# First products between the first modulation blocks, and the delta output projection begun with its ready inputs

## The chip, the cores and the metric

The kernel runs on one core of a Trainium2 chip. The time is device microseconds of one execution; the number that counts is the median of several. Times inside an execution are microseconds from the first instruction of the profiled one.

Engines: PE (TensorE, matrix products), ACT (ScalarE), DVE (VectorE), POOL (GpSimd), SP (SyncE, which here only issues DMA). Each runs its own instructions in order and waits for semaphores that the others raise.

## The reference

Two transformer blocks over 512 latent tokens of width 1024 (the first block also carries 256 context tokens, 768 columns in all), everything in float32. Only two places matter here. The start of the first block, layer 0 of 2:

```python
shift, scale, gate = jnp.split((c_act @ w_mod + b_mod)[:, None, :], 3, axis=-1)
lat = split_cols((rms_norm(h, norm_g) * (1.0 + scale) + shift) @ w_in)
```

(the same for the context with its own vector), and, in the second block, the end of the gated delta branch and the output projection of its mixing stage:

```python
o = o * lax.rsqrt(jnp.mean(o * o, axis=-1, keepdims=True) + EPS) * g_out
o = o * jax.nn.silu(gate)
mix = jnp.concatenate([attn_o, dn_o], axis=-1) @ w_out[l]
```

Half of the input of that last product, `attn_o`, is the window attention's output and has been finished long before the delta recurrence ends.

## The kernel before, in words

**Layout.** The stream is held with the 1024 features on 8 tiles of 128 partitions and the tokens in the free dimension. A weight chunk is 128 x 1024 float32 (512 KB): the eight 128 x 128 blocks that make one output tile. SP streams all chunks through `ring`, five places, in a fixed order; chunk c goes out only when chunk c - 5 is used (`chunk_used`). The order at the start is: parameters, chunk 0, all constants (1089 KB), then chunks 1 to 4 alternating with the four quarters of the tokens (768 KB each), then chunks as places come free.

**Split products.** A product is made exact enough by three passes: weights and inputs are split in a rounded "lead" and a rest, and PE adds lead x lead, lead x rest and rest x lead. The weight's lead is an ACT copy (`weight_leads`, L736) into one of two places of `scratch` or, for a few chunks in `LEAD_SPOTS`, a place of its own; its rest is a POOL subtraction in place (L564). A lead in `scratch` must wait until the chunk that used the place before is done. The input's split is a DVE cast (L1247) and subtraction (L1249), or an ACT copy (L761) and a DVE subtraction (L1474).

**The start.** Sixteen chunks hold the shift and scale columns of `w_mod`. A block b is two chunks. For each, PE makes two `modulation_part`s (L1995, a row of 256 sums), ACT copies the row out (`modulation_row`, L718), and PE turns it into columns (`modulation_turn`, L2005, which needs the constants). Beside them goes the first norm: ACT squares a token tile (L695), PE sums it over partitions (`norm_step`, L2012). The loop over b has one norm step per block from b = 2 on. After the last, ACT makes the root (L686, L687), and DVE makes the shifts and scales of all tiles at once (`modulation`, L1228 and L1232). Then, for each of the 8 tiles k, DVE multiplies by the root (L1467), ACT applies shift and scale (`modulate`, L757), and the result is split. `project_two` (L1957) makes the first two output tiles of the input projection together, tile k by tile k as the splits arrive, 12 matmuls for each k. Its weights are chunks 20 and 21 of the ring, behind four chunks of later modulation blocks; two of those blocks, of the 16 left, are made ahead of `project_two`.

**The end of the delta branch.** The recurrence has four steps s. After it, ACT squares each of the four heads (L1143), PE sums (L2584, into `pair_ps`), ACT makes the root (L686, L687), and DVE multiplies by root, gain and gate (L1770, L1771) and splits (L1247, L1249). Between the roots ACT makes the leads of the first two output chunks (L736) and POOL their rests. Then comes the output projection "out_2": eight output tiles, each 24 matmuls over eight input tiles (L1900, `project_split`). Input tiles 0 to 3 are the window attention's, 4 to 7 the delta heads. The order of all work is the order in which the code issues it; there is no scheduler.

## Time and profile before

| | us |
|---|---|
| median of 3 runs | 1842.37 |
| lowest, highest | 1839.61, 1842.48 |
| the profiled execution | 1841.66 |
| span of its instructions | 1839.8 |
| mean granted TensorE clock | 0.979 |

A row of the timeline reads: start, duration, engine, line, operation, tile written <- tiles read, shape, count, and in brackets how long the engine had been idle and who released it. A row of the chain of waits reads: start, duration, what the end of the execution hung on in that stretch. "L1957" is line 1957 of the kernel before.

### The profile page before, as it was taken

What the parts mean: (1) busy time and instruction counts of PE and PEld (TensorE: products, weight loads), DVE (VectorE), ACT (ScalarE), POOL (GpSimd) and SP (SyncE); (2) the same over time, 40 slices, a digit from 0 to 9 for tenths busy, and PEclk for the clock granted to TensorE, in tenths of its full rate; (3) what the DMA queues carried; (4) which work ended last, traced back from release to release, by engine and by line L of the source; (5) the groups of instructions that cost most, each with busy time, mean ns of one, the idle gap of its engine ahead of it and who ended that gap; (6) DMA issues with size and microseconds to landing.
All of it is one profiled execution on the core that took longest, in us unless ns stands there. A gap on an engine that the chain in (4) does not pass through costs nothing.

```text
span 1839.8 us, 32525 instructions
## 1 busy us (share of the span) xinstructions
PE 1701.1 (92%) x13658; PEld 1370.7 (74%) x13658; DVE 839.7 (46%) x1513; ACT 712.4 (39%) x1101; POOL 606.2 (33%) x318
## 2 busy tenths in 40 slices
PE   6899999988989989989999988788899899999997
PEld 3788888866878767768877757686688688888886
DVE  0401265475330356476747567574434444444113
ACT  3525213254353524354634966014423522222222
POOL 0222322193323323453034304113235244444443
PEclk9899999999999999999999989999999999999999
DMA  8344311210122111403522200001121132222232
GB/s 335 127 163 146 115 48 47 106 46 13 64 96 69 58 58 59 138 1 102 178 88 92 80 24 2 4 2 54 58 73 47 51 107 95 92 93 102 94 104 78
DMA packets 43721, 152.20 MB, mean 83 GB/s; under 512 B 4544, under 2 KB 7744, under 8 KB 43328
## 3 DMA queue, kind: packets, MB, share of 16 engines
q1 hardware_dynamic: 40032, 140.73, 22.1%
q10 hardware_dynamic: 3552, 9.47, 1.4%
q8 instruction: 108, 1.77, 0.4%
q14 instruction: 29, 0.24, 0.1%
HBM read 145.98 MB, written 4.19 MB: 82 GB/s over the span
## 4 chain that ended last, share of the span: by engine, by line
PE 78%; DVE 11%; ACT 6%; issue 4%; DMA 1%; SPq 0%; POOL 0%; DVEq 0%; ACTq 0%
PE wide_ps L1900 53%; PE wide_ps L1957 4%; PE pair_ps L2012 2%; PE wide_ps L2192 1%; PE wide_ps L1973 1%; PE wide_ps L2495 1%; DVE xn L1383 1%; DMA ring<-weights 1%; DVE xn L1628 1%; DVE proj L1301 1%; PE duo_ps L1995 1%; PE duo_ps L2622 1%; DVE proj L1297 1%; PE wide_ps L2078 1%; PE wide_ps L2603 1%
## 5 line engine op out<-in xcount | busy, mean ns | idle before, releaser
L564 POOL TENSOR_TENSOR ring_r<-ring,scratch_r 128x1024 fp32r<-128x1024 f32 x176 | 430.9, 2449 | 961.9 <-ACT scratch_r L736 887.5
L1900 PE MATMUL wide_ps<-xn_r,scratch_r 128*128 128x512 f32 x1272 | 470.3, 370 | 0.0
L1900 PE MATMUL wide_ps<-work_r,scratch_r 128*128 128x512 f32 (+1 forms) x1109 | 427.5, 386 | 5.2 <-ACT proj L723 5.2
L1900 PE MATMUL wide_ps<-work_r,ring_r 128*128 128x512 f32 (+1 forms) x1109 | 412.6, 372 | 0.0
L736 ACT ACTIVATE scratch_r<-ring 128x1024 fp32r<-128x1024 f32 x192 | 203.6, 1061 | 529.4 <-PE wide_ps L1900 461.5
L1900 PEld LDWEIGHTS wide_ps<-xn_r,scratch_r 128*128 128x128 f32 x1272 | 240.4, 189 | 47.5 <-issue 5.4
L1900 PEld LDWEIGHTS wide_ps<-work_r,scratch_r 128*128 128x128 f32 x1109 | 209.0, 188 | 53.5 <-ACT proj L723 9.9
L1900 PEld LDWEIGHTS wide_ps<-work_r,ring_r 128*128 128x128 f32 x1109 | 209.1, 189 | 38.6
L1900 PE MATMUL wide_ps<-proj_r,scratch_r 128*128 128x512 f32 (+1 forms) x662 | 225.7, 387 | 2.5 <-DVE proj_r L1249 2.5
L1900 PEld LDWEIGHTS wide_ps<-proj_r,scratch_r 128*128 128x128 f32 x662 | 125.4, 190 | 30.7 <-DVE proj_r L1249 3.3
L723 ACT ACTIVATE proj<-wide_ps 128x512 f32<-128x512 f32 (+2 forms) x86 | 56.7, 659 | 208.1 <-PE wide_ps L1900 198.4
L1420 DVE TENSOR_TENSOR work<-work 128x512 f32<-128x512 f32 (+2 forms) x35 | 36.4, 1039 | 124.3 <-ACT work L695 123.5
L1354 DVE SCALAR_TENSOR_TENSOR proj<-proj,par_sb,qe 128x768 f32<-128x768 f32 (+1 forms) x6 | 5.6, 930 | 184.4 <-ACT qe L687 184.4
L1900 PE MATMUL wide_ps<-proj_r,ring_r 128*128 128x512 f32 x188 | 75.0, 399 | 0.0
L1900 PE MATMUL wide_ps<-conv_tmp_r,ring_r 128*128 128x512 f32 (+1 forms) x179 | 66.4, 371 | 0.0
L1900 PE MATMUL wide_ps<-conv_tmp_r,scratch_r 128*128 128x512 f32 (+1 forms) x179 | 66.4, 371 | 0.0
L1440 DVE TENSOR_TENSOR h<-h,work 128x768 f32<-128x768 f32 (+1 forms) x16 | 29.8, 1863 | 65.2 <-ACT work L925 65.2
L1957 PE MATMUL wide_ps<-work_r,proj_r 128*128 128x512 f32 (+1 forms) x98 | 45.4, 463 | 12.4 <-DVE xn_r L1249 10.7
L1247 DVE CAST proj_r<-proj 128x512 fp32r<-128x512 f32 x24 | 51.8, 2160 | 0.8
L1808 DVE TENSOR_TENSOR proj<-wide_ps,work 128x512 f32<-128x512 f32 x30 | 20.6, 691 | 54.9 <-PE wide_ps L1900 38.5
L890 ACT ACTIVATE work<-pair_ps 128x512 f32<-128x512 f32 x52 | 31.0, 598 | 35.8 <-PE pair_ps L2215 35.8
L2215 PE MATMUL pair_ps<-const_sb,xn 128*128 128x128 f32 x208 | 31.2, 286 | 13.8 <-DVE xn L1383 7.8
(442 smaller groups left out, 2972.6 us busy)
## 6 DMA issues: line engine op xcount, KB each, us to landing
ring<-weights SPq DMA_DIRECT2D x256, 512.0 KB, 3.5
h<-tokens SPq DMA_DIRECT2D x4, 768.0 KB, 11.5
h<-tokens ACTq DMA_DIRECT2D x1, 3072.0 KB, 10.0
out<-h ACTq DMA_DIRECT2D x1, 2048.0 KB, 7.2
h<-out ACTq DMA_DIRECT2D x1, 2048.0 KB, 9.2
out<-h SPq DMA_DIRECT2D x16, 128.0 KB, 1.7
const_sb<-const SPq DMA_DIRECT2D x1, 1089.0 KB, 6.0
h<-mem ACTq DMA_DIRECT2D x1, 1024.0 KB, 12.7
```

The costliest lines, as they stand in the source:

```text
L564: pool.tensor_tensor(as_r(wt), wt, as_r(w_lead(m)).bitcast(F32), ALU.subtract).then_inc(w_split, 1)
L723: act.activation(dst, wide_ps[0:rows, g % 2 if bank is None else bank, 0:w], func).then_inc(evacuated, 1)
L736: act.activation(as_r(w_used(stage, w_lead(m))), w_used(stage, ring[:, c % RING, :]), ACT.Copy).then_inc(w_lead_ready, 1)
L890: act.activation(pair_probs_t(p)[:, 512 * q:512 * q + 512], turn_bank(g), ACT.Copy).then_inc(at_pt, 1)
L1247: dve.tensor_copy(as_r(lead), src).then_inc(x_lead, 1)
L1420: dve.tensor_tensor(total, total, squares(n)[:, k % 2, 0:w], ALU.add).then_inc(sq_used, 2 if k == 1 else 1)
L1440: dve.tensor_tensor(h[:, n, 0:w], h[:, n, 0:w], resid[:, n % 2, 0:w], ALU.add).then_inc(h_ready, 1)
L1808: dve.tensor_tensor(dst, proj_bank(stage, tile), root[:, 0:LAT], ALU.mult).then_inc(evacuated, 1)
L1900: last = pe.matmul(bank[:, a:b], wt[:, cols], as_r(x[:, a:b]), start=n == 0 and p == 0, stop=n == len(k_order) - 1 and p == 2)
L1957: last = pe.matmul(ps[:, a:b], wt[:, cols], as_r(x[:, a:b]), start=k == 0 and p == 0, stop=k == KT - 1 and p == 2)
L2012: last = pe.matmul(pair_ps[:, a:b], cst["ones"], squares(n)[:, k % 2, a:b], start=k == 0, stop=k == KT - 1)
L2215: last = pe.transpose(turn_bank(g)[:, t * P:(t + 1) * P], pair_probs(p - 1)[:, 512 * q + t * P:512 * q + (t + 1) * P], cst["ident"])
```

## The change

**Start, columns.** The modulation columns are laid out on the host by tile, so that block b holds shift and scale of token tile b alone. `first_modulation(b)` on DVE makes that tile's numbers as soon as block b is turned, and `modulate` waits for them tile by tile.

**Start, order of PE.** All eight norm steps go between the first three blocks; blocks 3, 4 and 5 follow; blocks 6 and 7 go inside `project_two`, behind its k = 0 and k = 1, and the first two of the later blocks behind k = 4 and k = 6.

**Start, ACT.** `modulation_row` is called for rows 0 and 1 ahead of the first and the fifth square, for 2 and 3 behind the root and the two weight leads, and for 4 to 9 behind tiles 0, 1, 2, 3, 5 and 7 of `modulate`.

**Start, DMA.** Constants go in two parts: 160 KB with identity, ones and the turning columns behind chunk 0, 960 KB with the tables behind chunk 7. The weights of the first two output tiles leave the ring: each has a place in `proj` and a semaphore of its own and is issued behind chunk 5 and chunk 6.

**out_2.** Its first two leads get places of their own in `xn` (`LEAD_SPOTS`), and ACT makes them behind step s = 1 of the recurrence. PE makes output tile 0 over input tiles 0 to 3 ahead of the first two head sums, output tile 1 over the same ahead of the last two, and input tiles 4 to 7 for both together afterwards (`out_part`).

```diff
-    for name, n in ([("mod0", MOD_FIRST), ("proj0", NPROJ + 2 * MIXED), ("dft0", FOURIER_CHUNKS[0]), ("out0", KT),
+    for name, n in ([("mod0", MOD_FIRST), ("proj0", NPROJ - 2 + 2 * MIXED), ("dft0", FOURIER_CHUNKS[0]), ("out0", KT),
...
+        ROWS_BEHIND = {0: 4, 1: 5, 2: 6, 3: 7, 5: KT, 7: KT + 1}
...
                 if c == 0:
-                    sp.dma_start(const[:, :], const_d).then_inc(const_landed, 16)
+                    sp.dma_start(const[:, 0:CONST_HEAD], const_d[:, 0:CONST_HEAD]).then_inc(const_landed, 16)
+                if c in (5, 6):
+                    sp.dma_start(w_home("proj0", c - 5), weights[where("proj0", c - 5)]).then_inc(first_landed[c - 5], 16)
+                if c == 7:
+                    sp.dma_start(const[:, CONST_HEAD:], const_d[:, CONST_HEAD:]).then_inc(tables_landed, 16)
...
             def modulate(ly):
-                act.wait_ge(mod_ready, (2, 4)[ly])
                 for k in range(KT):
-                    if ly == 0 and k == 1:
-                        modulation_row(KT + 1)
-                        weight_leads("proj0", 1)
+                    act.wait_ge(mod_ready, (2 * (k + 1), 2 * KT + 2)[ly])
...
+                    if ly == 0 and k in ROWS_BEHIND:
+                        modulation_row(ROWS_BEHIND[k])
...
                     for k in range(KT):
-                        modulation_row(k)
+                        if k in (0, 4):
+                            modulation_row(k // 4)
                         act.wait_ge(tokens_landed[k // 2], 16)
                         square(0, k, h[:, k, :], TOK)
                     mean_root(0, TOK)
-                    weight_leads("proj0", 0)
-                    modulation_row(KT)
+                    weight_leads("proj0", 0, 2)
+                    modulation_row(2)
+                    modulation_row(3)
...
+                if s == 1:
+                    weight_leads("out_2", 0, 2)
...
-                if n in (1, 2):
-
-                    weight_leads("out_2", n - 1)
...
+            def first_modulation(b):
+
+                dve.wait_ge(mod_turned, b + 1)
...
+            def first_block(b):
+
+                pe.wait_ge(mod_row, b - 1)
+                if b == 4:
+                    pe.wait_ge(root_ready, 1)
                 modulation_part(0, 2 * b)
+                modulation_turn(b - 1)
+                if b == 2:
+                    norm_step(0, 6, TOK)
+                    norm_step(0, 7, TOK)
                 modulation_part(0, 2 * b + 1)
...
+            def behind_first_products(k):
+
+                if k < 2:
+                    first_block(6 + k)
+                elif k == 2:
+                    modulation_turn(KT - 1)
+                elif k == 4:
+                    late_block(KT)
+                elif k == 6:
+                    modulation_turn(KT)
+                    late_block(KT + 1)
...
+            def out_part(tiles, ks):
...
             for n in range(4):
+                if n % 2 == 0:
+                    out_part([n // 2], range(4))
                 pe.wait_ge(do_sq, n + 1)
...
-            for n in range(KT):
-                project_split("out_2", n, range(KT), mix2_lead, lambda k: tile_2[:, MIX2[k], :], LAT, mix2_ready if n == 0 else None)
+            out_part([0, 1], range(4, KT))
+            for n in range(2, KT):
+                project_split("out_2", n, range(KT), mix2_lead, lambda k: tile_2[:, MIX2[k], :], LAT)
```

On PE, the program's start before (L1995 is a half block, L2005 a turn, L2012 a norm step in two matmuls, of 512 and of 256 columns):

```order
L1995 MATMUL wide_ps<-ring,state 32x256 x12
L2005 MATMUL duo_ps<-const_sb,work 128x2 x2
L1995 MATMUL wide_ps<-ring,state 32x256 x8
L2005 MATMUL duo_ps<-const_sb,work 128x2 x2
L1995 MATMUL wide_ps<-ring,state 32x256 x4
L2012 MATMUL pair_ps<-work,const_sb 128x512
L2012 MATMUL pair_ps<-work,const_sb 128x256
L1995 MATMUL wide_ps<-ring,state 32x256 x4
L2005 MATMUL duo_ps<-const_sb,work 128x2 x2
L1995 MATMUL wide_ps<-ring,state 32x256 x4
```

and now (L2037, L2049 and L2056 are the same three):

```order
L2037 MATMUL wide_ps<-ring,state 32x256 x8
L2056 MATMUL pair_ps<-work,const_sb 128x512
L2056 MATMUL pair_ps<-work,const_sb 128x256
L2056 MATMUL pair_ps<-work,const_sb 128x512
L2056 MATMUL pair_ps<-work,const_sb 128x256
L2037 MATMUL wide_ps<-ring,state 32x256 x4
L2049 MATMUL duo_ps<-const_sb,proj 128x2 x2
L2056 MATMUL pair_ps<-work,const_sb 128x512
L2056 MATMUL pair_ps<-work,const_sb 128x256
L2056 MATMUL pair_ps<-work,const_sb 128x512
L2056 MATMUL pair_ps<-work,const_sb 128x256
L2037 MATMUL wide_ps<-ring,state 32x256 x4
```

The norm steps now stand two at a time ahead of half blocks that they stood behind.

On ACT, from the root of the first norm to the fourth token tile of `modulate`, now (L709 and L710 the root, L765 the weight leads, L741 the copy of a row, L783 the modulation of a tile in two pieces, L787 its lead):

```order
L709 ACTIVATE work<-pair_ps,eps 128x768 [waits sq_used]
L710 ACTIVATE work<-work 128x768 [waits act_chain]
L765 ACTIVATE proj_r<-proj 128x1024 [waits first_landed0]
L765 ACTIVATE proj_r<-proj 128x1024 [waits first_landed1]
L741 ACTIVATE proj<-wide_ps 128x256 [waits mod_turned,chunk_used] x2
L783 ACTIVATE xn<-xn,small 128x512 [waits scaled,mod_ready]
L783 ACTIVATE xn<-xn,small 128x256
L741 ACTIVATE proj<-pair_ps 128x256 [waits mod_turned,chunk_used]
L783 ACTIVATE xn<-xn,small 128x512 [waits scaled,mod_ready]
L783 ACTIVATE xn<-xn,small 128x256
L787 ACTIVATE work_r<-xn 128x768 [waits xn_ready]
L741 ACTIVATE proj<-pair_ps 128x256 [waits mod_turned,chunk_used]
```

Before, rows 0 to 7 were all copied ahead of L709; now six of them stand behind it.

On PE, the end of the recurrence before (L2577 its last products, L2584 the head sums, L1900 the projection):

```order
L2577 MATMUL duo_ps<-work,xn 128x128 x8
L2584 MATMUL pair_ps<-work,const_sb 128x512 x4
L1900 MATMUL wide_ps<-proj_r,scratch_r 128x512 x2
L1900 MATMUL wide_ps<-proj_r,ring_r 128x512
L1900 MATMUL wide_ps<-proj_r,scratch_r 128x512 x2
```

and now (L2654, L2679 and L2668 the same; the rows from the third are output tile 0 over input tiles 0 to 3):

```order
L2654 MATMUL duo_ps<-work,xn 128x128 x8
L2668 MATMUL wide_ps<-proj_r,xn_r 128x512 x2
L2668 MATMUL wide_ps<-proj_r,ring_r 128x512
L2668 MATMUL wide_ps<-proj_r,xn_r 128x512 x2
L2668 MATMUL wide_ps<-proj_r,ring_r 128x512
L2668 MATMUL wide_ps<-state_r,xn_r 128x512
L2668 MATMUL wide_ps<-proj_r,xn_r 128x512
L2668 MATMUL wide_ps<-state_r,ring_r 128x512
L2668 MATMUL wide_ps<-qe_r,xn_r 128x512
L2668 MATMUL wide_ps<-proj_r,xn_r 128x512
L2668 MATMUL wide_ps<-qe_r,ring_r 128x512
L2679 MATMUL pair_ps<-work,const_sb 128x512 x2
```

Twelve products of output tile 0 stand ahead of the first head sum, twelve of tile 1 ahead of the third.

## Rows read from the trace of the kernel before

**Rows 1.** The page: busy time of the engines, share of the span, instructions.

```profile
PE 1701.1 (92%) x13658; PEld 1370.7 (74%) x13658; DVE 839.7 (46%) x1513; ACT 712.4 (39%) x1101; POOL 606.2 (33%) x318
```

**Rows 2.** Chain of waits, 0 to 75 us: start, duration, what (x counts trace records).

```profile
6.46 15.37 DMA ring<-weights
...
21.88 1.08 PE wide_ps L1995 x8
22.96 2.58 PE pair_ps L2012 x4
25.53 0.57 PE wide_ps L1995 x8
26.10 0.54 PE duo_ps L2005 x4
...
27.21 1.49 PE pair_ps L2012 x4
...
44.41 0.91 ACT work L686
...
53.85 19.45 PE wide_ps L1957 x96
```

**Rows 3.** Timeline of PE, its last two waits before the first products.

```profile
47.46 0.61 PE L2005 MATMUL duo_ps<-const_sb,proj 128*128 128x2 f32 x4 [2.08 <-ACT proj L718]
...
53.85 0.77 PE L1957 MATMUL wide_ps<-work_r,proj_r 128*128 128x512 f32 x1 [4.79 <-DVE xn_r L1249]
```

**Rows 4.** Timeline of ACT, 45 to 53 us.

```profile
45.34 0.84 ACT L687 ACTIVATE work<-work 128x768 f32<-128x768 f32 x1
46.09 1.04 ACT L736 ACTIVATE proj_r<-ring 128x1024 fp32r<-128x1024 f32 x1
47.04 0.36 ACT L718 ACTIVATE proj<-duo_ps 128x256 f32<-128x256 f32 x1
47.30 1.30 ACT L757 ACTIVATE xn<-xn,small 128x512 f32<-128x512 f32 x2
...
51.69 0.85 ACT L761 ACTIVATE work_r<-xn 128x768 fp32r<-128x768 f32 x1
```

**Rows 5.** Timeline of DVE, 46 to 58 us.

```profile
46.22 1.83 DVE L1467 TENSOR_TENSOR xn<-h,work 128x768 f32<-128x768 f32 x2 [4.09 <-ACT work L687]
48.64 2.05 DVE L1247 CAST work_r<-xn 128x768 fp32r<-128x768 f32 x1 [0.59 <-ACT xn L757]
50.72 2.99 DVE L1249 TENSOR_TENSOR xn_r<-xn,work_r 128x768 fp32r<-128x768 f32 x1
...
56.23 0.55 DVE L1247 CAST conv_tmp_r<-xn 128x768 fp32r<-128x768 f32 x1
56.82 0.96 DVE L1249 TENSOR_TENSOR xn_r<-xn,conv_tmp_r 128x768 fp32r<-128x768 f32 x1
```

**Rows 6.** Timeline of POOL, its first weight rest.

```profile
47.21 3.05 POOL L564 TENSOR_TENSOR ring_r<-ring,proj_r 128x1024 fp32r<-128x1024 f32 x1 [45.99 <-ACT proj_r L736]
```

**Rows 7.** Windows of PE: stretch, length, PE busy (records), granted clock, DMA share, GB/s.

```profile
53.85:57.83 3.98, 3.98 (x13) 0.50 0.02 4
57.83:61.63 3.80, 3.80 (x20) 0.81 0.00 0
```

**Rows 8.** Chain of waits, 1240 to 1304 us.

```profile
1240.17 1.86 PE duo_ps L2577 x16
...
1243.46 1.14 PE pair_ps L2584 x2
...
1247.52 2.48 DVE proj_r L1247
...
1250.03 2.72 DVE proj_r L1249
...
1260.54 41.45 PE wide_ps L1900 x171
```

**Rows 9.** Line L1808, DVE reading PSUM: count, ns min/median/max, first and last start.

```profile
L1808 DVE TENSOR_TENSOR proj<-wide_ps,work x30: 678/692/692, 1330.5 to 1698.8; 128x512 f32<-128x512 f32 x30
```

157 lines of the change are left out of this document (104 added, 53 removed).

## The prediction, made before the changed kernel had run

> **What bounds the kernel now.** The busy shares come first: PE works 92% of the span, no other engine half of it [rows 1]. So the time is PE's work plus PE's waits, and an edit is worth what it takes out of those waits (or of stretches at the lower clock) and nothing else. The chain of waits then says where they lie. In the first 54 us it leaves PE three times [rows 2]. First for the DMA: chunk 5, issued at 6.46, lands 15.37 us later, behind all constants and tokens. Then for the root at 44.41, after a run of PE work that is continuous from 21.88. Then for the first input tile: the products of `project_two` start at 53.85, after idle times of 2.08 and 4.79 us [rows 3], and run 19.45 us to 73.30. Windows of PE show the price behind the second wait: granted clock 0.50 for the first 3.98 us, which hold the 12 matmuls of k = 0, and 0.81 in the next [rows 7]. At the end of the recurrence PE finishes at 1242.03 and the full stream of the output projection starts at 1260.54 [rows 8]; between them stand squares, sums, roots and a DVE chain, in which a cast takes 2.48 us and a subtraction 2.72.
>
> **Prices, from rows.** Half block 0.57 us at the high clock (1.08 at the low one), turn 0.54, norm step 1.49 (2.58 low) [rows 2]. ACT: root 0.91 + 0.84, weight lead 1.04, row copy 0.36, modulating a tile 1.30, its lead 0.85 [rows 2, 4]. DVE: root product 1.83 / 2 = 0.92, cast 0.55, subtraction 0.96 [rows 5]. One k of `project_two`: 3.98 at the low clock [rows 7]; at the high one (73.30 - 61.63) / 5.5 = 2.12, since 61.63 lies half way through k = 2 [rows 2, 7].
>
> **Start, until the root.** The first constants shrink from 1089 to 160 KB. Up to chunk 5 the queue moved about 7.5 MB by 21.83, or 0.37 MB per us [rows 2]; 0.95 MB less puts the last tokens and chunk 5 about 2.6 us earlier, near 18 and 19. The two first weight chunks follow at about 20.6 and 23.4. PE can sum tiles 0 and 1 from about 10 us on, at the low clock (to 15), then half block 2, norm steps 2 and 3, half block 3 (to 20.1). ACT holds row 1 until that half block is done, so square 4 ends at 21.5; steps 4 and 5 end at 24.5, half block 4 and turn 1 at 25.6, steps 6 and 7 at 28.6, half block 5 at 29.2. Root: 28.6 + 0.91 + 0.84 = **30.4**, against 46.2 before. Fifteen us earlier, but not fifteen us won, since blocks 3 to 7 are still to come.
>
> **From the root to the first products.** ACT queues two weight leads ahead of row 2: it is out at 30.4 + 2.1 + 0.4 = 32.8. PE has finished half block 6 at 29.8 and waits 3.0 us for it: a wait that the change adds, with all blocks queued behind it. Then turn 2, half blocks 7 and 8, turn 3 (35.1), half blocks 9 and 10 (36.2), turn 4 (behind row 4, which stands behind `modulate` of tile 0, out at 36.2), half block 11 at 37.3. For the input: DVE multiplies tile 0 to 31.4, then waits for turn 2 to make tile 2's scales, then turn 3 for tile 3's; ACT has tile 0 at 35.8. POOL meanwhile makes the two weight rests. Before, DVE's cast took 2.05 instead of 0.55 and its subtraction 2.99 instead of 0.96 exactly while POOL ran [rows 5, 6]: the two stop each other. Here POOL runs from 31.5 to about 37.3, so the cast of tile 0 starts then, and its split is ready at **39.0**. PE waits 1.7 us. It would be 37.6 without the collision.
>
> **Inside `project_two`.** Eight k at 2.12 are 17.0. Added to it: blocks 6 and 7 (4 x 0.57), turns 5, 6, 7 (3 x 0.54), two later blocks (2 x 1.1) and their turn (0.4), in all 6.5. These are no new work, only moved. Two waits more. Row 8 stands on ACT behind the later block that PE makes after k = 4; tile 6 is modulated only behind it (ACT 54.9 to 56.2), cast and subtracted by 57.8, while PE has finished k = 5 at 56.5: 1.3 us. DVE has eight small instructions more than before in the loop, 0.4 us for each tile, which hold splits back by a few tenths (k = 4) that fit in the same sum: 0.2. End of the products: 39.0 + 17.0 + 6.5 + 1.3 = **63.8** (the turn that follows at 73.30 before follows here too). Before it was 73.30, with the same work done by then. **Gain 9.5 us.** What follows is PE without a break, so the shift lasts. The wait for the tables (landed near 27) costs nothing, nor do the ring's waits: chunk 12 can go out at 34 with half block 7, and is needed at 41.
>
> Bounds of this term: without the POOL collision +1.4, with a little less waiting in the loop 11.2. The clock: after the wait of 2.08 us PE went on at the high level, after 4.79 at the low one [rows 2, 3, 7]; the new one of 3.0 lies between. If the clock falls there and again at 37, half blocks and turns cost 2 us more and k = 0 1.9 us more: 5.6. The rise before took most of 5.4 us of products. I take the high level, as the gap is nearer to 2.08.
> On this, the Trainium skill ("TensorE: Matmul & The Clock Gate", section "What's actually happening") says that throttled is the default and that activity releases it. By that rule alone either level can stand after 3.0 us; it would put the gain between 5.6 and 9.5.
>
> **out_2.** Before, from the end of the recurrence: output of the last step on DVE, square, head sum 1.14, root, then for each head about 2.6 us on DVE, of which head 0 lost (2.48 - 0.44) + (2.72 - 0.69) = 4.1 to POOL's two weight rests [rows 8]. Output tile 0 hung on head 3's split until 1260.54, and then came 171 matmuls in 41.45 us: 0.232 each at the high clock, 39.7, and 1.7 for a start at the low one.
> Now PE puts 12 matmuls (2.8 us) ahead of head sum 0, which then ends at 1245.8 instead of 1244.6: 1.2 lost on DVE's chain, since the square is ready at 1243.4. ACT has no leads between the roots, and POOL is quiet: head 0 is split at 1249.8 (1252.75 before), head 1 at 1252.4. Head sums 2 and 3 stand behind 12 matmuls of tile 1, to 1249.6; the sums end at 1250.6 and 1251.6, the roots at 1251.9 and 1253.3: no delay for heads 2 and 3. But the lead of chunk 2 no longer waits for a product, because the place in `scratch` is free: ACT makes it at 1253.3 to 1254.4, and POOL's rest follows, from 1255.05, when head 2's subtraction ends, to 1257.4. Head 3's chain stands behind it: 1257.4 + 2.6 = 1260.0 instead of 1257.6. So the collision of rows 8 is not gone, it is halved and moved. From there 6 + 144 matmuls, 34.8, and 1.7 for the clock, as PE idles 3.6 us before: 1296.5, against 1260.54 + 41.45 = 1302.0. **Gain 5.4 us.**
> The two early rests run on POOL beside the recurrence's third step. DVE's instructions there read PSUM and one tile of SBUF; such an instruction takes 678 to 692 ns in all 30 cases, among POOL's rests [rows 9]. I take nothing for it; at worst it is two rests, 4.8. ACT's two leads (2.1 us) fall into an idle time of over 7 us. Bounds: if head 3 escapes POOL, 34.8 from 1257.6 and no low clock, 9.5; if the recurrence pays 4.8, 0.6.
>
> **Sum.** 1841.66 - 9.5 - 5.4 = 1826.8 for the profiled execution; the median of the runs shown is 0.7 above it: **1827.5**.
>
> **Rivals.**
> *A. POOL and DVE do not meet again* (at 1255, or at 35): the starting times are within a microsecond of each other, so it can fall out so. 9.5 for 5.4, perhaps 1.4 more: 1822 to 1823. For it: the order on DVE and POOL is settled by tenths. Against: I see the lead of chunk 2 freed at once. 0.17.
> *B. The clock falls in the new gaps* (3.0 us at 29.8, 1.7 at 37.3): 1831, or up to 1833 if more of the products pay. 0.14.
> *C. The early rests hold the recurrence:* 4.8 of the 5.4 is lost: 1832. Against it rows 9. 0.06.
> *D. The gain doesn't last:* the stage behind the first products waits for something with a time of its own. The DMA would be it: PE's next stage wants three chunks per 9.9 us. Against: the ring runs two chunks ahead of before. Within 0.2% only if out_2 fails too. 0.04, 1837 to 1842.
> *E. Slower.* PE stays at the low clock through the whole interleaved stretch, because each short wait meets a row, a scale or a split. Eight k at 3.98 are 31.8, 14.8 more; the moved blocks and turns 6 more; end near 84, some 3 of it hidden in waits for splits: 81, that is 8 lost where 9.5 was won. With out_2's 5.4 won: 1845. It decides from about 70% of the stretch at the low level. Against: from 53.85 the same products rose within 5.4 us, and the waits inside the loop are 1.3 and less.
> The Trainium skill's section "HAM oscillation — how this bites in real kernels" on the same page tells of bursts of products with waits between them that start low every time; this is what would make E, and no trace of before shows it here. 0.03.
>
> **How the numbers follow.** Forecast, with both terms near what is worked out: 0.56. Range of the forecast alone: 1824 to 1830. The range reaches to A, B and C: **1821 to 1833**. These cases hold 0.93, but each scatters by a microsecond or two about its time, so I count the range for little over 0.8. Runs of this kernel can't tell less than about 0.2% (3.7 us) from no change. Faster by more than that: all but D and E, 0.93; within 0.04; slower 0.03.
>
> **What will show it.** In the profile after: root ready near 30.4; a PE wait of about 3 us for row 2 behind half block 6; the first L1997 (the products) near 39 and its last near 63.8, clock 1.00 in between; a wait of about 1.3 us ahead of k = 6. Root at 30 but products ending past 67 would mean that rows and scales, not the root, set the pace. In out_2: head sum 0 a microsecond later than before against the end of the recurrence, head 0 split 3 us earlier, one POOL rest in the middle of the four head chains, and the projection's end 5 to 6 us closer to the recurrence's end. The recurrence itself must take as long as before. A stretch outside these two places that changes by more than 2 us would be outside this argument.

## The result, and the profile after

The changed kernel takes **1815.14 us** (median of 4, 1813.44 to 1815.88) where the kernel before took 1842.42 in the same comparison (1839.61 to 1844.11). The ratio is 0.9854, 95% interval 0.9841 to 0.9867. The forecast was 1827.5 with a range of 1821 to 1833: the direction was right, and the time came out 12 us under the forecast and 6 under the range. The two profiled executions are 1839.8 and 1814.1 us long, 25.7 apart, and that difference is what has to be found.

**The page.** Busy time of the engines, share of the span and instructions of the kernel after:

```profile
PE 1689.6 (93%) x13658; PEld 1372.4 (76%) x13658; DVE 838.4 (46%) x1527; ACT 710.1 (39%) x1101; POOL 604.7 (33%) x318
```

Against [rows 1] this is the first odd thing. The same 13658 matmuls were issued, and PE is busy 11.5 us less. A change that only takes out waits leaves the busy time alone, and the mean granted clock is nearly the same (0.979 before, 0.977 now).

**The start.** Chain of waits of the kernel after, 0 to 70 us (start, duration, what; x counts records):

```profile
27.75 0.91 ACT work L709
...
29.43 1.99 ACT proj_r L765 x2
31.42 0.28 ACT proj L741
...
31.74 0.61 PE duo_ps L2049 x4
...
38.98 3.90 PE wide_ps L1997 x12
42.88 0.57 PE pair_ps L2037 x8
...
44.56 2.30 PE wide_ps L1997 x12
...
58.74 0.97 DVE xn_r L1285
...
59.75 2.35 PE wide_ps L1997 x12
...
65.74 0.34 PE duo_ps L2049 x4
```

The chain goes through the root (ready near 29.5), the two weight leads, row 2, the blocks, and then the products, `project_two`, from 38.98 to 65.74. Before, they ran from 53.85 to 73.30 [rows 2]. So 14.9 us earlier at the first product, 7.56 at the last. The first k takes 3.90 us, a later one 2.1 to 2.4. The windows of PE say why (stretch, length, PE busy with records, granted clock, DMA share, GB/s):

```profile
28.70:31.70 3.00, 0.01 (x3) 1.00 0.92 284
31.70:38.90 7.20, 7.16 (x52) 0.54 0.74 257
38.90:42.80 3.90, 3.90 (x16) 0.54 0.77 299
42.80:65.80 23.00, 22.00 (x168) 1.00 0.47 157
```

PE idled 3.0 us for row 2, and half a microsecond behind that the granted clock falls to the lower of its two levels (1.2 of 2.4 GHz; 0.54 is the mean of a window that holds a little of the high level too), until near 42.8. The timeline of PE has the two waits of this stretch, with what ended them:

```profile
31.74 0.61 PE L2049 MATMUL duo_ps<-const_sb,proj 128*128 128x2 f32 x4 [3.03 <-ACT proj L741]
...
59.75 0.50 PE L1997 MATMUL wide_ps<-work_r,proj_r 128*128 128x512 f32 x1 [0.99 <-DVE xn_r L1285]
```

DVE and POOL, in their timelines, hardly meet at the first tile. On DVE a small multiplication for the scales of tile 3, then the cast of tile 0 and its subtraction:

```profile
35.39 0.64 DVE L1268 SCALAR_TENSOR_TENSOR small<-small,par_sb 128x2 f32<-128x2 f32 x1
35.95 0.55 DVE L1283 CAST work_r<-xn 128x768 fp32r<-128x768 f32 x1
36.53 0.96 DVE L1285 TENSOR_TENSOR xn_r<-xn,work_r 128x768 fp32r<-128x768 f32 x1
```

and POOL's two rests, which end at 36.01:

```profile
30.55 5.46 POOL L587 TENSOR_TENSOR proj_r<-proj,proj_r 128x1024 fp32r<-128x1024 f32 x2 [29.33 <-ACT proj_r L765]
```

The small multiplication ends with the rests, after 0.64 us; with POOL quiet the same takes 0.16 (at 38.47). This half microsecond is all that the meeting costs here; cast and subtraction have their usual lengths.

**out_2.** The chain again, 1225 to 1290 us:

```profile
1231.30 1.84 PE duo_ps L2654 x16
1233.14 2.77 PE wide_ps L2668 x12
1235.92 0.87 PE pair_ps L2679 x2
...
1240.17 0.69 DVE proj_r L1285
...
1245.33 2.72 DVE proj_r L1285
...
1248.10 5.50 PE wide_ps L2668 x12
1253.60 33.02 PE wide_ps L1940 x144
```

POOL's rests in the same stretch, two beside the recurrence and one among the head chains:

```profile
1215.57 4.68 POOL L587 TENSOR_TENSOR ring_r<-ring,xn_r 128x1024 fp32r<-128x1024 f32 x2 [11.24 <-ACT xn_r L765]
1244.92 2.57 POOL L587 TENSOR_TENSOR ring_r<-ring,scratch_r 128x1024 fp32r<-128x1024 f32 x1 [24.67 <-ACT scratch_r L765]
```

The recurrence ends at 1233.14, the output projection at 1286.62: 53.48 us between them. Before it was 1242.03 to 1301.99, or 59.96 [rows 8].

**The rest.** From there to the end neither the code nor the order of the work differs, and yet it takes 527.5 us instead of 537.8. The three longest unbroken runs of matmuls in the chain, of the kernel before:

```profile
1335.98 27.82 PE wide_ps L1900 x120
...
1397.86 44.49 PE wide_ps L1900 x192
...
1476.13 335.30 PE wide_ps L1900 x1446
```

and of the kernel after:

```profile
1319.80 27.21 PE wide_ps L1940 x120
...
1381.10 43.58 PE wide_ps L1940 x192
...
1457.23 328.22 PE wide_ps L1940 x1446
```

These matmuls of 512 columns followed each other every 231.7 ns (44.49 / 192) and now every 227.0 (43.58 / 192); taken from their starts between 1500 and 1600 us it is 231.67 and 226.67. No engine is waited for inside these runs, and both have the full clock. The three runs together are 8.6 us shorter, of the 10.3. The whole difference of 25.7 us is then:

| stretch | before | after | gain | forecast |
|---|---|---|---|---|
| to the end of the first products | 73.30 | 65.74 | 7.56 | 9.5 |
| to the end of the recurrence | 1168.73 | 1167.40 | 1.33 | 0 |
| out_2 | 59.96 | 53.48 | 6.5 | 5.4 |
| from there to the end | 537.8 | 527.5 | 10.3 | 0 |

### The profile page after: what moved, and what is told of

Read it like the earlier page. It is cut to its first block, busy times and chain, and to the rows that moved or that the text cites. A ratio compares the mean times of both kernels' runs of the same rounds, so it can differ in the third digit from the quotient of the medians.

```text
span 1814.1 us, 32562 instructions
## 1 busy us (share of the span) xinstructions
PE 1689.6 (93%) x13658; PEld 1372.4 (76%) x13658; DVE 838.4 (46%) x1527; ACT 710.1 (39%) x1101; POOL 604.7 (33%) x318
## 4 chain that ended last, share of the span: by engine, by line
PE 79%; DVE 10%; ACT 6%; issue 4%; DMA 0%; POOL 0%; SPq 0%; DVEq 0%; ACTq 0%
PE wide_ps L1940 52%; PE wide_ps L1997 4%; PE pair_ps L2056 2%; PE wide_ps L2236 1%; PE wide_ps L2015 1%; PE wide_ps L2572 1%; DVE xn L1419 1%; PE duo_ps L2037 1%; DVE xn L1668 1%; ACT xn L906 1%; PE wide_ps L2122 1%; PE duo_ps L2718 1%; DVE proj L1337 1%; PE wide_ps L2593 1%; PE wide_ps L2699 1%
## 5 line engine op out<-in xcount | busy, mean ns | idle before, releaser
L587 POOL TENSOR_TENSOR ring_r<-ring,scratch_r 128x1024 fp32r<-128x1024 f32 x174 | 425.2, 2444 | 942.9 <-ACT scratch_r L765 870.5
L765 ACT ACTIVATE scratch_r<-ring 128x1024 fp32r<-128x1024 f32 x190 | 200.8, 1058 | 502.4 <-PE wide_ps L1940 441.1
L1940 PE MATMUL wide_ps<-proj_r,scratch_r 128*128 128x512 f32 x634 | 212.3, 380 | 0.0
L1940 PEld LDWEIGHTS wide_ps<-proj_r,scratch_r 128*128 128x128 f32 x634 | 119.4, 188 | 22.6
L1940 PE MATMUL wide_ps<-proj_r,ring_r 128*128 128x512 f32 x176 | 68.5, 389 | 0.0
L1997 PE MATMUL wide_ps<-work_r,proj_r 128*128 128x512 f32 (+2 forms) x126 | 50.5, 435 | 8.6 <-DVE xn_r L1285 6.9
## 6 DMA issues: line engine op xcount, KB each, us to landing
h<-tokens ACTq DMA_DIRECT2D x1, 3072.0 KB, 10.3
h<-mem ACTq DMA_DIRECT2D x1, 1024.0 KB, 12.2
```

The source lines that it names most:

```text
L587: pool.tensor_tensor(as_r(wt), wt, as_r(w_lead(m)).bitcast(F32), ALU.subtract).then_inc(w_split, 1)
L765: act.activation(as_r(w_used(stage, w_lead(m))), w_used(stage, w_home(stage, i)), ACT.Copy).then_inc(w_lead_ready, 1)
L1940: last = pe.matmul(bank[:, a:b], wt[:, cols], as_r(x[:, a:b]), start=n == 0 and p == 0, stop=n == len(k_order) - 1 and p == 2)
L1997: last = pe.matmul(ps[:, a:b], wt[:, cols], as_r(x[:, a:b]), start=k == 0 and p == 0, stop=k == KT - 1 and p == 2)
```

## The experiments

Times are medians in us with their range, and the kernel before is the one measured beside them; a single execution is marked as one. The rates are worked out from the starts of the matmuls between 1500 and 1600 us, unless another stretch is named.

### Each part alone

`out2_only` is the kernel before with only the edits of the output projection.

```diff
+                if s == 1:
+                    weight_leads("out_2", 0, 2)
...
+                if n % 2 == 0:
+                    out_part([n // 2], range(4))
```

> The kernel before with the out_2 part of the change alone (its two early weight leads, out_part, the removed leads between the roots). By the forecast this part is worth 5.4 us: 1837. Theory A (what made the changed kernel faster than forecast is the rate of PE: 512-column matmuls follow each other in 226.7 ns there and in 231.7 ns before, over about 2160 of them, and that rate goes with where PE's instructions lie in its stream): this kernel has PE's instructions moved only from out_2 on, so the stages ahead of it stay at 231.7, and those behind may go either way: 1837 at 231.7, 1827 at 226.7. Theory B (the rate is set by what happens in the first 70 us, by the way PE's stream starts): all stages stay at 231.7, 1837.

1836.43 (1834.82 to 1837.64) against 1842.19: ratio 0.9974, interval 0.9964 to 0.9984, so 4.8 us by the ratio and 5.8 by the medians. Rate 231.67 ns. The term of the sum was 5.4.

`start_only` is the changed kernel with the output projection as before.

```diff
-                if s == 1:
-                    weight_leads("out_2", 0, 2)
+                if n in (1, 2):
+                    weight_leads("out_2", n - 1)
```

> The changed kernel with the out_2 part taken back. By the forecast the start is worth 9.5 us; its products end 7.6 us earlier in the changed kernel's trace. Theory B: the faster rate (226.7 ns) comes with the start: 7.6 + 1.3 + 10.3 = 19.2 us less than before, 1823, and 226.7 ns in the last product stages. Theory A: the stages up to out_2 run as in the changed kernel; behind it the rate may be either: 1823 or 1833.

1820.89 (1820.52 to 1821.24), ratio 0.9891, interval 0.9871 to 0.991. That is 21.3 us under the kernel before, more than twice what was forecast for the start, and the late stages run at 226.67 ns. The two parts add up (27.1 against 27.3), and the quicker matmuls come with the start part, though nothing in it touches the stages that gain.

### Two harmless shifts: not the cause

The start part also changes the number of instructions and of semaphores. `one_more` puts one wait more at the head of PE's program:

```diff
+            pe.wait_ge(par_landed, 16)
             pe.wait_ge(ready, 3)
```

> The kernel before with one wait more at the start of PE's program, on a semaphore that has long been raised: every instruction of PE behind it stands one place later in its stream, nothing else changes. Theory A: the spacing of 512-column matmuls can change from 231.7 ns: some 10 to 12 us less if it goes to 226.7 everywhere. Theory B: nothing changes, 1842, 231.7 ns.

One execution: 1841.78, rate 231.66. `four_sems` takes four semaphores that nothing uses:

```diff
+        unused = [sem(f"unused{n}") for n in range(4)]
```

> The kernel before with four semaphores more that nothing uses, so that those behind have the numbers that they have in the changed kernel. Theory C (the numbers of the semaphores, which every waiting or signalling instruction carries, set the rate): 226.7 ns somewhere, up to 12 us less. Theories A and B: nothing changes, 1842.

One execution: 1842.24, rate 231.68. Neither does anything to the rate.

### The padding of the table

What was left is a piece of the diff that the prediction had passed over, and that its text doesn't show. The small constants that the first blocks need are put at the head of the table, and a padding fills them up:

```diff
-                             ("dft_ch", 2 * P), ..., ("pick", 2)])
+CONST_COLS, N_CONST = table([("ident", P), ("ones", P), ("pick", 2), ("pad", 62), ("ones_head", P), ...
```

The table grows from 2178 to 2240 columns, or from 8712 to 8960 bytes in each partition. In SBUF the tensors lie one behind another in the order h, xn, proj, ring, const, work, scratch, state, qe_2, conv_tmp, each start rounded up to 32 bytes (as the code implies; no trace shows an address, and what the sizes in the code fix are the differences between the columns of the table below). All sizes but that of const are multiples of 256 bytes. So the old table displaces everything behind it against everything ahead of it. Where the tensors start, as remainders of 256 bytes:

| kernel | h, xn, proj, ring, const | work | scratch, state, qe_2, conv_tmp | 512-column matmul, ns |
|---|---|---|---|---|
| before | 128 | 160 | 160 | 231.67 |
| after, pad_62 | 128 | 128 | 128 | 226.67 |
| after_unpadded | 128 | 160 | 160 | 231.67 |
| gap_scratch | 128 | 160 | 128 | 232.53 |
| work_alone | 128 | 128 | 160 | 231.67 |
| pad_14 | 128 | 192 | 192 | 233.34 |
| pad_30 | 128 | 0 | 0 | 231.11 |
| front_32 | 0 | 0 | 0 | 226.67 |
| const_last | 128 (const 128, last) | 128 | 128 | 226.67 |

`pad_62` is the kernel before with the padding and nothing else:

```diff
-                             ("dft_ch", 2 * P), ..., ("pick", 2)])
+                             ("dft_ch", 2 * P), ..., ("pick", 2), ("pad", 62)])
```

> The kernel before with 62 columns of zeros put behind its table of constants, and nothing else: the table takes 8960 bytes a partition instead of 8712, so everything that lies behind it in SBUF (work, scratch, state, qe_2, conv_tmp and the small tensors) starts 224 bytes further on, at a multiple of 64 bytes and no longer 32 bytes past one. Theory D (placement): the 512-column matmuls follow each other every 226.7 ns instead of 231.7 from layer 1 on, worth 21.5 (before less start_only) less the 7.6 to 8.9 that the products and the blocks themselves gained ahead of the recurrence's end, so 1842.4 - 11.6 to 12.6: about 1830.5, with layer 0's products unchanged in time. Theory E (the rate comes with something else that the start part brings, such as the second landing place of two chunks, the split table load or the freed bank): 1842.4, rate 231.7.

1831.45 (1830.3 to 1831.77) against 1840.83: ratio 0.9944, interval 0.9927 to 0.9961. The rate is 226.67. The window of PE from 1500 to 1600 us, first of the kernel before:

```profile
1500.00:1600.00 100.00, 100.00 (x433) 1.00 0.28 95
```

and of `pad_62`:

```profile
1500.00:1600.00 100.00, 100.00 (x442) 1.00 0.29 96
```

PE has no gap in either, the clock is full in both, and nine matmuls more go through the same 100 us. The arithmetic and its order are the same.

`after_unpadded` is the counterpart, the changed kernel without its 62 columns:

```diff
-("pick", 2), ("pad", 62), ("ones_head", P)
+("pick", 2), ("ones_head", P)
```

> The changed kernel without the 62 columns of padding that its new table of constants has, so that work, scratch and what follows lie where they lay in the kernel before; the loads and all the instructions are as in the changed kernel. Theory D (placement): the rate goes back to 231.7 ns and the time to 1815.1 + 11.6 = about 1826.7, close to the 1827.5 that was predicted. Theory E (something else of the start part): 1815, rate 226.7.

1827.38 (1827.05 to 1832.38), ratio 0.9933, interval 0.9914 to 0.9952. The window and the long runs are those of the kernel before:

```profile
1321.88 27.82 PE wide_ps L1940 x120
...
1383.76 44.49 PE wide_ps L1940 x192
```

Against the changed kernel's median, which is of another comparison, the 62 columns are worth 12.2 us; by `pad_62` they are worth 9.4. What the prediction had described, without them, lands 0.1 us from the predicted 1827.5; that is closer than its terms deserve (below).

By stages, from the starts of the same matmuls in the traces, the padding doesn't only give. `pad_62` is 1.1 us behind the kernel before at 354 us, 2.4 behind at the end of the recurrence, and level at the end of out_2; all its gain, 10.0 us, comes after that. `after_unpadded` needs 536.3 us from the end of out_2 to the end, where the kernel before needs 537.8 and the changed kernel 527.5. So 8.8 of the 10.3 us of that stretch are the padding's by this pair, and 1.5 are won at the old pace; what wins them isn't known.

### Which tensors, and which places

`gap_scratch` moves scratch and what follows to the changed kernel's places and leaves work where it was; `work_alone` does the reverse (the table padded by 62, and 8 unused columns ahead of scratch).

```diff
                   "work": [P, 8, TOK],
+                  "gap": [P, 56],
                   "scratch": [P, 2 * CHUNK],
```

> The kernel before with 56 unused columns between work and scratch: work stays 32 bytes past a multiple of 64, but scratch (where the rounded weights of most chunks lie), state, qe_2, conv_tmp and the small tensors move to the very addresses of the changed kernel. If the weights' place sets the rate: 1830.5 and 226.7 ns. If the place of the activations in work does: 1842 and 231.7 ns. A mixture of two rates by stage would say that both count. If theory D is wrong altogether: 1842.

> The kernel pad_62 with 8 more columns between work and scratch: work lies at a multiple of 128 bytes, and scratch, state, qe_2, conv_tmp 32 bytes past one; the counterpart of gap_scratch, which had it the other way round and was at 232.5 ns in the gate and up products (work, scratch and ring are read there) and 226.85 in the down products (proj with scratch and ring). If a matmul is quick only where both its weights and its input lie at a multiple of 128: about 231 to 232 ns in both stages, and a time near 1842. If one of the two were enough, the gate and up products would be at 226.7 here, about 5 us less: 1837.

One execution each: 1839.98 and 1844.63. `gap_scratch` separates by what a matmul reads. Groups of PE, line by form, 1500 to 1600 us (out<-inputs and weights, count, busy us and mean ns of one):

```profile
L1902 PE MATMUL wide_ps<-xn_r,scratch_r 128*128 128x512 f32 x144 | 56.5, 392 | 0.0
L1902 PE MATMUL wide_ps<-work_r,scratch_r 128*128 128x512 f32 x126 | 50.2, 398 | 0.0
L1902 PE MATMUL wide_ps<-work_r,ring_r 128*128 128x512 f32 x126 | 49.6, 394 | 0.0
L1902 PE MATMUL wide_ps<-conv_tmp_r,ring_r 128*128 128x512 f32 x18 | 7.0, 389 | 0.0
```

and the same view from 1745 to 1795 us, in the down projection:

```profile
L1902 PE MATMUL wide_ps<-proj_r,scratch_r 128*128 128x512 f32 x140 | 43.8, 389 | 0.0
```

Where work is among the operands, a record lasts 394 to 398 ns; conv_tmp with ring, which lie alike, has 389, as all have in the changed kernel. xn with scratch lie alike too and have 392: their matmuls stand in the stream next to those that read work. In the down projection, where work isn't read, the rate is 226.85 although the kernel as a whole is no quicker. `work_alone` has 231.67 in the first stretch and 231.9 from 1700 to 1750 us, in the down projection, since scratch holds most of the weights. Both kinds of operand count, and one group of tensors out of place is enough to slow the stream. A rule for a single pair doesn't come out of the records: conv_tmp with scratch, alike in each case, has 398 ns before (both at 160) and 388 in `work_alone` (both at 160), 398 in `pad_30` (both at 0) and 389 in `front_32` (both at 0). What its neighbours in the stream read counts as well.

`pad_14` and `pad_30` ask how far out of place is too far:

> The kernel before with 14 columns of zeros behind its table of constants: work, scratch and what follows move by 32 bytes, to a multiple of 64 that is no multiple of 128. If a multiple of 64 bytes is enough: 1830.5, rate 226.7 ns. If it must be a multiple of 128: 1842, rate 231.7 ns. Theory E: 1842 and 231.7 as well, and then pad_62 shows it too.

> The kernel before with 30 columns of zeros behind its table of constants: work and scratch start at a multiple of 256 bytes, where pad_62 and the changed kernel have them 128 bytes past one (as h, xn, proj and ring lie in all of them). If a multiple of 128 bytes is what counts: the late stages run at 226.7 ns a 512-column matmul and the time is about 1831.5, that of pad_62. If work and scratch must lie as the other tensors do, 128 bytes past a multiple of 256: 231 to 233 ns and 1842 to 1848, as pad_14 (64 bytes past a multiple of 128: 233.3 ns, 1848).

One execution each: 1848.19 at 233.34 ns, and 1842.41 at 231.11 ns (233.07 from 1700 to 1750 us). So work and scratch at a "rounder" place, 0, are slow while the others lie at 128. `front_32` then moves all of them there:

```diff
-        shapes = {"h": [P, KT, TOK],
+        shapes = {"gap": [P, 32],
+                  "h": [P, KT, TOK],
```

> pad_62 with 32 unused columns (128 bytes) ahead of h: every tensor that matmuls read then starts at a multiple of 256 bytes, as work and scratch alone did in pad_30. If only the places of the operands relative to each other count: 226.7 ns and about 1831.5, as pad_62. If the absolute place counts: 231 to 233 ns and about 1842, as pad_30.

One execution: 1829.3, rate 226.67.

```profile
1500.00:1600.00 100.00, 100.00 (x443) 1.00 0.30 99
```

**At these two common remainders, 128 and 0, only the place of the operands relative to each other counts.** A third one wasn't run. `const_last` needs no padding at all:

```diff
-                  "const_sb": [P, N_CONST],
...
-                  "conv_tmp": [P, TOK]}
+                  "conv_tmp": [P, TOK],
+                  "const_sb": [P, N_CONST]}
```

> The kernel before with its table of constants unchanged (2178 columns, no padding) but placed behind conv_tmp, so that work, scratch, state, qe_2 and conv_tmp follow on ring, 128 bytes past a multiple of 256. If only the place counts: 226.7 ns and about 1831.5, as pad_62. If the table's padding itself does something: 231.7 ns and 1842.

One execution: 1827.99, rate 226.67. The table is the old one to the byte, so the padding does nothing but shift what follows. In this kernel work lies 20480 bytes behind the start of ring, in `pad_62` 29440, and the difference is an odd multiple of 256. So a shift by 256 bytes costs nothing, where one by 128 does (`pad_30`).

### The wait for row 2, and the wait for row 8

`row_2_first` takes away most of the 3.03 us wait that the change adds:

```diff
-                    weight_leads("proj0", 0, 2)
                     modulation_row(2)
+                    weight_leads("proj0", 0, 2)
```

> The changed kernel with ScalarE taking row 2 of the modulation out of its bank ahead of the two weight leads, and no longer behind them. The leads' 2.0 us then lie behind 0.36 us of the row, so TensorE's wait of 3.03 us at 31.7 ends about 1.8 us earlier, as 1.1 us or less. Theory B (the clock falls in that gap, and the slow stretch to 42.9 follows from it): with the shorter gap the clock may stay at its high level, and the half blocks, the turns and k=0 of the products are then 3 to 4 us shorter; but k=0 can't begin before tile 0 is split at 37.5 (38.9 now), so the gain is the 1.4 us there and some 1.3 us of k=0 at the high clock: 1812.4. If the clock falls all the same: 1.4 us at most: 1813.7. Against it: the rests on GpSimd begin 0.4 us later and then lie beside VectorE's cast of tile 0, which could hold k=0 at 38.9: 1815.1.

1818.14 (1816.82 to 1820.24), ratio 0.9875, interval 0.9855 to 0.9894: no gain over the changed kernel, rather 3 us worse. PE in the timeline:

```profile
30.53 0.61 PE L2049 MATMUL duo_ps<-const_sb,proj 128*128 128x2 f32 x4 [1.14 <-ACT proj L741]
...
38.29 0.76 PE L1997 MATMUL wide_ps<-work_r,proj_r 128*128 128x512 f32 x1 [1.17 <-DVE xn_r L1285]
```

The wait is down to 1.14 us as expected, but a wait for tile 0 has taken its place. DVE and POOL tell why:

```profile
35.15 3.00 DVE L1285 TENSOR_TENSOR xn_r<-xn,work_r 128x768 fp32r<-128x768 f32 x1
```

```profile
31.50 5.83 POOL L587 TENSOR_TENSOR proj_r<-proj,proj_r 128x1024 fp32r<-128x1024 f32 x2 [30.28 <-ACT proj_r L765]
```

The leads begin a microsecond later and the modulation of tile 0 is ready 1.2 us earlier, so the subtraction of tile 0 now lies beside POOL's second rest and takes 3.00 us instead of 0.96. The root was 0.7 us later in this execution; the products start 0.7 us earlier than in the changed kernel and end at 65.84, where it had 65.74. The clock falls all the same, as the windows of PE show:

```profile
33.20:38.30 5.10, 3.93 (x30) 0.51 1.00 377
38.30:42.40 4.10, 4.10 (x13) 0.50 0.44 178
```

From the products' end to 214 us the two profiled executions are 0.1 us apart. Then this one loses 1.6 us in 3.4, where the code is the same, because the granted clock is 0.50 from 214.2 to 217.6 and 1.00 there in the changed kernel. It doesn't belong to the edit: `row_8_later` and `after_unpadded`, which leave row 2 where it was, lose the same 1.6 us in the same place. The window of `row_8_later`:

```profile
211.80:215.20 3.40, 3.40 (x15) 0.50 0.10 39
```

What makes the clock fall there in three of the traces and not in the others isn't known. That leaves the edit no gain and the rest of the 3 us in the medians unexplained.

`row_8_later` takes out the other wait:

```diff
-        ROWS_BEHIND = {0: 4, 1: 5, 2: 6, 3: 7, 5: KT, 7: KT + 1}
+        ROWS_BEHIND = {0: 4, 1: 5, 2: 6, 3: 7, 6: KT, 7: KT + 1}
```

> The changed kernel with row 8 taken out behind the modulation of tile 6, as in rows_2_and_8, and the leads ahead of row 2, as in the changed kernel. If the 1.3 us that rows_2_and_8 showed behind the products over row_2_first are row 8's alone: 1815.1 - 1.3 = 1813.8. If the rest of its 3.6 us against the changed kernel comes from row 8 as well: 1811.5.

1813.79 (1813.2 to 1814.57), ratio 0.9842, interval 0.9824 to 0.986. In the chain k = 5 and k = 6 now stand in one piece, and the products end at 63.67, of which 0.8 us were already won at the root, ahead of anything that the edit touches:

```profile
55.65 4.38 PE wide_ps L1997 x24
60.03 0.34 PE duo_ps L2049 x4
```

`rows_2_and_8` makes both edits:

> row_2_first, and with it row 8 is taken out behind the modulation of tile 6 and not ahead of it: ScalarE waits 4.14 us for row 8 ahead of tile 6 in the changed kernel (56.5), and TensorE waits 0.99 us for tile 6 behind that (59.75). With tile 6 modulated first that wait goes, and tile 7 must then be there by the end of k=6 and its late block: 1.0 us less than row_2_first, about 1811.5; if tile 7, now modulated behind row 8, comes too late in its place, no gain over row_2_first.

1811.55 (1810.97 to 1811.99), ratio 0.9834, interval 0.9816 to 0.9852: 3.6 us under the changed kernel and, with the next, the quickest here. `row_8_later` is 1.3 under the changed kernel, with ranges that overlap (1813.2 to 1814.57, 1813.44 to 1815.88); what is shown of row 8 is that the wait of 0.99 us is gone. In the profiled execution of `rows_2_and_8` the products end 1.3 us earlier than in the changed kernel. The rest of its lead, 2.5 us, arises between 400 and 500 us and behind 1150, where the code is the same, and isn't explained.

`rows_and_place` is `rows_2_and_8` with the unpadded table placed last, as in `const_last`:

> rows_2_and_8 without the 62 columns of padding, and with the table of constants placed behind conv_tmp. All matmul operands again lie 128 bytes past a multiple of 256, so the rate is 226.7 ns. If place alone is what the padding was for: 1811.5, that of rows_2_and_8, within 1 us. If the table's place behind ring has a cost of its own, as the one run of const_last may show (3.5 us under pad_62): about 1808. If the padding is needed for something else: 1821 or more.

1811.06 (1807.92 to 1813.46). No price of the table's place shows, and the low single time of `const_last` is within the scatter of 5 us that these four executions have. The profiled one is the quickest, 1807.92. It has the waits of 1.14 and 0.56 us of `row_2_first` in the same places and one of 2.74 for tile 0 behind them, and yet the clock stays high until the products have begun:

```profile
29.50:38.00 8.50, 5.09 (x55) 1.00 0.98 368
38.00:41.40 3.40, 3.40 (x18) 0.50 0.38 155
```

Its products end at 62.74, 1.7 us ahead of those of `rows_2_and_8`, whose instructions are the same: 0.9 of it was there at the root, and the rest came under the shorter stretch of the low clock.

## Why the prediction was right or wrong, point by point

**The step that failed is a term that the sum puts at nothing.** 1841.66 - 9.5 - 5.4 has no term for any stretch but the two that the change edits. The constants' edit was costed as a shorter first load, that is, by what it moves in time, and at nothing for what it moves in space. The forecast rested on a PE that does the same matmuls in the same time: "What follows is PE without a break, so the shift lasts." It did last, and on top of it each 512-column matmul of the later stages got 5 ns shorter. Behind out_2, where the changed kernel gains 10.3 us, the padding makes 8.8 of them by `after_unpadded`, and 10.0 by `pad_62`. In out_2 itself it makes some 0.6 of 6.5 (`after_unpadded` gains 5.9 there). Whether the 1.33 us between the first products and the recurrence's end are its work isn't shown: `pad_62` loses 2.1 us over that stretch, and `after_unpadded` wins 0.4. By the medians the padding as a whole is worth 9.4 us (`pad_62`) and 12.2 (`after_unpadded`). The prediction had named its own test: "A stretch outside these two places that changes by more than 2 us would be outside this argument." That test fired.

**Root ready near 30.4:** 29.5. Right within a microsecond.

**A wait of 3.0 us for row 2:** 3.03. Right, and behind it the clock fell, which was rival B. The forecast took the high level, since 3.0 lay nearer to 2.08 (high afterwards) than to 4.79 (low afterwards) [rows 3, 7]. That misread the kernel before, whose windows had only been taken from 53.85 on. Windows of PE, kernel before:

```profile
47.40:49.00 1.60, 1.54 (x20) 1.00 1.02 415
49.00:53.80 4.80, 0.06 (x4) 0.50 0.67 242
```

The clock fell at 49.0, 1.5 us behind the end of the wait of 2.08 and as the wait of 4.79 began, so it can't have been that long wait that brought it down. In `row_2_first` it falls at 33.2 behind waits of 1.14 and 0.56 us, and in `rows_and_place` it stays high behind the same two. The length of the last wait alone doesn't tell the level.

**Tile 0 split at 39.0 because POOL and DVE meet; PE waits 1.7 us:** the start of the products is right by luck. The cast did begin as the rests ended, but they ended at 36.01 and not at 37.3; they held DVE for half a microsecond, and tile 0 was split at 37.5. PE was late itself, its half blocks and turns at the low clock taking 1.0 each instead of 0.57 and 0.54, and began the products at 38.98. PE waited for nothing. Two errors of about 1.5 us cancelled. `row_2_first` shows the meeting that the forecast had described, with the 2.99 us of [rows 5] measured as 3.00.

**39.0 + 17.0 + 6.5 + 1.3 = 63.8:** 65.74. The term is mis-sized by 1.9. The wait ahead of k = 6 was 0.99 for 1.3. The first k took 3.90 instead of 2.12, which is 1.8 and nearly the whole error; the forecast's own price for it, 1.9, stood under "the clock". So the start gave 7.56 us and not 9.5.

**out_2: 5.4:** `out2_only` 4.8 to 5.8; right. By steps: head sum 0 was 0.9 + 2.8 us behind the recurrence's end, as worked out. Head 0 was split at 7.7 us behind it (forecast 7.8). One rest of POOL fell among the head chains, at 1244.92, that is 11.8 us behind the recurrence's end (forecast 13.0), so it caught head 2's subtraction (2.72 instead of 0.69) and not head 3's. PE's 12 matmuls on head 2 then ran at the low clock, 5.50 us, and head 3's chain hid behind them. The end at 53.5 us behind the recurrence, or 54.1 at the old rate (`after_unpadded`), was forecast as 54.5. On this collision the Trainium skill's page "SBUF — State Buffer", section "Who interferes with whom", says that a VectorE instruction with two inputs in SBUF contends with a GpSimd one that reads SBUF; the rows agree, with 2.72 against 0.69.

**Rival A**, that POOL and DVE don't meet again, came true, but for half a microsecond, at the first tile, where PE was late anyway, and not in out_2, where the chain runs through head 2's subtraction of 2.72 us.

**The early rests and the recurrence (rival C):** nothing. Both rests ran beside it (4.68 us from 1215.57), and the recurrence's shift is the same at 1212 and at its end. **Rival D**, a gain that doesn't last: no, by the starts of the same matmuls. The shift is 4.4 us at the least, near 403 us, at the end of a stretch (397.4 to 404.2, clock 0.50) whose work the kernel before does at the high clock; it is over 5.3 everywhere else behind 68 us. **Rival E**, slower by the low clock throughout: no. From 42.8 to 65.8 the clock is 1.00.

**What of the sum is confirmed.** Without the padding the change is worth 13.5 us (by the medians, interval 8.8 to 15.8 by the ratio), where 14.9 was forecast. The sum was about right for what it contained, as a whole: in that trace the start gave 6.7 us (for 9.5), out_2 5.9 (for 5.4), and the other stretches 1.9 that the sum didn't have. The range, which was made from the same terms, had no room for what it didn't.

## What to carry to other kernels

An edit that changes the size of a buffer moves every buffer allocated behind it: before costing it at nothing, read where the matmul operands start, and give all tensors that a stream of matmuls reads, weights and inputs, the same remainder of 256 bytes (128 and 0 are what was run here). It is worth an experiment of its own, since in the stages with 768 columns the same places cost 0.8 us. In a kernel that is PE-bound, compare PE's busy time at an equal number of instructions, and the length of an unbroken run at an equal count, before looking for waits. A short wait that is removed ahead of two engines which block each other is worth only what their new order leaves of it.

## What was not expected of the hardware

- TensorE's rate depends on where its operands lie. With all weights and inputs of the stream at the same remainder of 256 bytes, 128x512 products follow each other every 226.67 ns, with work and scratch 32 bytes off the others at 231.67, 64 off at 231 to 233.3, 128 off at 231.1 to 233.1. It is relative as far as was run: remainders of 128 throughout and of 0 throughout give 226.67 alike. Why this is so is open; where the results lie in PSUM wasn't varied. The Trainium skill's page "SBUF — State Buffer", section "Who interferes with whom", says that PE never waits on anyone. The rows don't speak against it, since nothing here shows another engine in it, but PE's pace does depend on the places in SBUF. That its two reads disturb each other would fit, and isn't shown.
- The gain is in later stages with 512 columns. In layer 0, where each weight tile goes with 768 columns in two pieces, it is a small loss: between 74 and 354 us the traces of the changed kernel, `start_only`, `pad_62`, `front_32` and `const_last` each lose 0.75 to 0.8 us on the kernel before, and those of `out2_only` and `one_more`, with the old places, lose nothing. Why isn't known.
- The Trainium skill's page "TensorE: Matmul & The Clock Gate", section "Back-to-back issue gap", gives a sustained 131 ns for such a product with its weight load. The traces disagree: of 24 such products in a row none here come under 226 ns each. The measurement decides for this kernel's type of data, fp32r.
- Traces of kernels whose code is the same in a stretch differ there by steps of 1.5 to 3 us (about 214 to 218, 650 to 820 and 1150 to 1210 us in the traces compared). The first of these steps is the granted clock's, 0.50 for 3.4 us in some traces and 1.00 in others; the others weren't followed up. A difference of that size in one trace says nothing yet.
